# Norm sums in two fp32r passes, softmax's last product on GpSimd, and consecutive splits of queries and keys

## The reference

```python
def rmsnorm_2(x, g):
    xf = x.astype(jnp.float32)
    y = xf * lax.rsqrt(jnp.mean(xf * xf, axis=-1, keepdims=True) + EPS)
    return (y * g.astype(jnp.float32)).astype(x.dtype)
...
q_ca = rmsnorm_2(hs(q_ca, N_CA_HEADS), g_q[l])
k_ca = rmsnorm_2(hs(k_ca, N_CA_HEADS), g_k[l])
...
s = jnp.einsum('bnqhd,bnkhd->bnhqk', qc, k_band).astype(jnp.float32) * (d ** -0.5)
s = s + bias[None, None]
p = jax.nn.softmax(s, axis=-1)
out = jnp.einsum('bnhqk,bnkhd->bnqhd', p.astype(v.dtype), v_band)
```

## Time and profile before

| | |
|---|---|
| median of three runs | 955.28 us (955.16 to 955.39) |
| the profiled execution | 955.42 us |
| its span in the profile | 953.7 us |
| busy: TensorE, VectorE, ScalarE, GpSimd | 941.1, 691.2, 565.2, 103.8 us |
| granted TensorE clock | 1.0 throughout, the upper level of 2.4 GHz |
| steps 0 to 63 | about 393 to 453 us |

### The profile page before, as it was taken

One profiled execution on the slowest core, in us unless ns is written; L12 is line 12 of the kernel. 1 busy time (PEld: TensorE's weight loads), 2 busy tenths in 40 slices (PEclk: granted clock), 3 DMA queues, 4 the chain that ended last, 5 costly groups with the idle time before them and its releaser, 6 DMA issues.

```text
span 953.7 us, 13305 instructions
## 1 busy us (share of the span) xinstructions
PE 941.1 (99%) x4712; PEld 786.3 (82%) x4712; DVE 691.2 (72%) x1278; ACT 565.2 (59%) x1115; POOL 103.8 (11%) x215
## 2 busy tenths in 40 slices
PE   8999999999999999999999999999999999999998
PEld 7878998888888887877788877898888888888887
DVE  6487888878788766667768886856544853673988
ACT  6448787753223257479987664556745634644562
POOL 5001212211121103000000000110000000000110
PEclk9999999999999999999999999999999999999999
DMA  8233222149798743733442423365867567586773
GB/s 302 89 112 108 69 79 89 55 157 354 284 322 278 190 142 127 300 111 100 133 166 73 127 67 131 146 167 133 212 207 180 168 192 189 122 234 193 169 186 111
DMA packets 34963, 156.71 MB, mean 164 GB/s; under 512 B 5273, under 2 KB 5529, under 8 KB 22226
## 3 DMA queue, kind: packets, MB, share of 16 engines
q1 hardware_dynamic: 21106, 103.64, 31.6%
q0 software_dynamic: 11152, 49.29, 20.9%
q10 hardware_dynamic: 2640, 2.93, 0.9%
HBM read 144.61 MB, written 5.27 MB: 157 GB/s over the span
## 4 chain that ended last, share of the span: by engine, by line
PE 86%; DVE 9%; ACT 3%; issue 1%; DMA 1%; ACTq 0%; POOL 0%; DVEq 0%; POOLq 0%
PE psum L2276 26%; PE psum L2278 25%; PE psum L2277 25%; PE psum L2423 2%; PE psum L2450 2%; PE psum L2479 1%; PE psum L2474 1%; DVE wl L1318 1%; DVE p_sb L1518 1%; DMA raw<-in_wall 1%; DVE ptl L1537 1%; PE psum L2712 1%; DVE hl L1357 1%; DVE xt L1353 1%; DVE ah L1464 1%
## 5 line engine op out<-in xcount | busy, mean ns | idle before, releaser
L2276 PE MATMUL psum<-hh,wh 128*128 128x512 f32 (+2 forms) x736 | 277.7, 377 | 0.7 <-DVE hl L1357 0.6
L2278 PE MATMUL psum<-hh,wl 128*128 128x512 f32 (+2 forms) x736 | 270.2, 367 | 0.0
L2277 PE MATMUL psum<-hl,wh 128*128 128x512 f32 (+2 forms) x736 | 270.0, 367 | 0.0
L1318 DVE TENSOR_TENSOR wl<-raw,wh 128x512 fp32r<-128x512 f32 x336 | 218.7, 685 | 37.6 <-ACT wh L733 37.0
L733 ACT ACTIVATE wh<-raw 128x512 fp32r<-128x512 f32 x336 | 193.3, 621 | 68.3 <-PE psum L2278 65.2
L2276 PEld LDWEIGHTS psum<-hh,wh 128*128 128x128 f32 x736 | 138.5, 188 | 24.5 <-DVE hl L1357 1.8
L2278 PEld LDWEIGHTS psum<-hh,wl 128*128 128x128 f32 x736 | 138.4, 188 | 23.0
L2277 PEld LDWEIGHTS psum<-hl,wh 128*128 128x128 f32 x736 | 138.7, 188 | 20.5 <-issue 1.2
L2276 PE MATMUL psum<-wh,ah 128*128 128x512 f32 x192 | 76.1, 396 | 0.4 <-ACT p_sb L879 0.4
L2278 PE MATMUL psum<-wh,al 128*128 128x512 f32 x192 | 74.9, 390 | 0.0
L2277 PE MATMUL psum<-wl,ah 128*128 128x512 f32 x192 | 74.8, 389 | 0.0
(11 more groups left out here) (372 smaller groups left out, 1748.6 us busy)
## 6 DMA issues: line engine op xcount, KB each, us to landing
raw<-in_wall SPq DMA_DIRECT2D x79, 1024.0 KB, 5.4
raw<-in_wall POOLq DMA_DIRECT2D x20, 1024.0 KB, 8.1
wa<-in_wada POOLq DMA_DIRECT2D x24, 512.0 KB, 5.8
gt<-in_wada POOLq DMA_DIRECT2D x20, 512.0 KB, 6.9
xt<-in_xcols SPq DMA_DIRECT2D x8, 264.0 KB, 7.9
cb<-c_rows SPq DMA_DIRECT2D x8, 264.0 KB, 3.2
x<-in_x SPq DMA_DIRECT2D x4, 512.0 KB, 11.9
x_kept<-x SPq DMA_DIRECT2D x4, 512.0 KB, 2.6
```

What stands on the lines that cost most here:

```text
L1318: e.tensor_tensor(lower_, raw_of(w, c), upper_.bitcast(F32), ALU.subtract).then_inc(v["wl"], 1)
L2276: e.matmul(out_, lh, rh, start=start, stop=False, skip_group_check=True)
L2277: e.matmul(out_, lh, rl, start=False, stop=False, skip_group_check=True)
L2278: return e.matmul(out_, ll, rh, start=False, stop=stop, skip_group_check=True)
```

## The change

The sum of squares. `blk` becomes fp32r. After the square, ScalarE copies it to an fp32r tile `sq_hi`; two steps after the square (`LAG_LOW`) VectorE subtracts that from the square into `sq_lo`; and the sum is two fp32r matmuls, of the upper and of the lower part. `LAG_SUM`, `LAG_ROOT` and `LAG_NORM` go from 2, 3, 4 to 4, 5, 6 steps. Both new tiles exist once, so each waits for the sum before. They lie in memory that is free in this stage.

Softmax's last product goes from ScalarE to GpSimd for heads 8 to 15, five beats behind the scores and not six, and TensorE's transposes wait for GpSimd. GpSimd now walks the list of steps too, with its table masks, the row and the strip in between.

The splits of softmax heads' queries and keys stand in steps 6, 7, 8 and 9 on ScalarE (before 6, 8, 10 and 12) and in 7, 8, 9 and 10 on VectorE (before 7, 9, 11 and 13). Semaphores are renamed.

```diff
-        blk = sb("blk", [128, 128])
+        blk = sb("blk", [128, 128], F32R)
...
-        LAG_SUM, LAG_ROOT, LAG_NORM = 2, 3, 4
+        LAG_LOW, LAG_SUM, LAG_ROOT, LAG_NORM = 2, 4, 5, 6
...
-                if (x_ := at(AGE["norm"])) and x_[0] == "S" and x_[1] not in SB:
+                if (x_ := at(AGE["norm"])) and x_[0] == "S" and x_[1] in FG:
                     normalize(*x_[1:])
...
-                if 16 <= n < 80 and k in (6, 8, 10, 12):
-                    p, part = 3 + n // 16, (k // 2 - 3) % 2
-                    if k < 10:
+                if 16 <= n < 80 and k in (6, 7, 8, 9):
+                    p, part = 3 + n // 16, k % 2
+                    if k < 8:
...
                     e.activation(sq[:, sub, :], bank[sub], ACT.Square).then_inc(a["sq"], 1)
+                    e.wait_ge(a["sq"], 4 * p + 2 * sub + 1)
+                    if p or sub:
+                        e.wait_ge(t["ss"], 2 * p + sub)
+                    e.activation(sq_hi, sq[:, sub, :], ACT.Copy).then_inc(a["sq"], 1)
...
+                if n - LAG_LOW in SQUARES:
+                    p, sub = SQUARES[n - LAG_LOW]
+                    e.wait_ge(a["sq"], 4 * p + 2 * sub + 2)
+                    if p or sub:
+                        e.wait_ge(t["ss"], 2 * p + sub)
+                    e.tensor_tensor(sq_lo, sq[:, sub, :], sq_hi.bitcast(F32), ALU.subtract).then_inc(v["ss"], 1)
...
-                if 16 <= n < 80 and k in (7, 9, 11, 13):
-                    p, part = 3 + n // 16, (k // 2 - 3) % 2
-                    if k < 10:
+                if 16 <= n < 80 and k in (7, 8, 9, 10):
+                    p, part = 3 + n // 16, (k - 7) % 2
+                    if k < 9:
...
-            for h in CA:
+            def table_mask(h):
                 e.wait_ge(d[f"bt{h % 2}"], 16 * (h // 2 - 3))
                 e.memset(bt[h % 2][0:64, 448:512], NEG).then_inc(g["bt"], 1)
...
+            def normalize(h, i):
+                mx, su, nmx = small(h, i)
+                e.wait_ge(v["rcp"], n_score(h, i))
+                e.tensor_scalar(block_p(h, i), block_p(h, i), mx, None, ALU.mult).then_inc(g["norm"], 1)
+
+            table_mask(8)
+            table_mask(9)
+            for n in range(steps_s):
+                if n == 31:
+                    first_value_row()
+                if n == 72:
+                    whole_sticks()
+                if n > 16 and n % 16 == 1:
+                    for x_ in beats_s[first_s[n - 17]:first_s[n - 1]]:
+                        if x_ and x_[0] == "S" and x_[2] == 0 and x_[1] + 2 in CA:
+                            table_mask(x_[1] + 2)
+                for b_ in range(first_s[n], first_s[n + 1]):
+                    x_ = beats_s[b_ - 5] if b_ > 4 else None
+                    if x_ and x_[0] == "S" and x_[1] in CA:
+                        normalize(*x_[1:])
...
+                elif h in CA:
+                    e.wait_ge(g["norm"], 12 + n_score(h, i0) - 32)
                 else:
                     e.wait_ge(a["norm"], n_score(h, i0))
...
-                    e.wait_ge(a["sq"], 2 * p + sub + 1)
+                    e.wait_ge(v["ss"], 1 + 2 * p + sub + 1)
...
-                    e.matmul(bank[2], blk[:, :], sq[:, sub, :], start=True, stop=True).then_inc(t["ss"], 1)
+                    e.matmul(bank[2], blk[:, :], sq_hi, start=True, stop=False)
+                    e.matmul(bank[2], blk[:, :], sq_lo, start=False, stop=True).then_inc(t["ss"], 1)
```

More of the change, by code:

```diff
@@ L205, in program @@
         br.close()
+        bq = ExitStack()
+        sb("under_q", [128, 3072], where=bq)
+        parts_q = sb("sq_parts", [128, 2, SEQ], F32R, where=bq)
+        bq.close()
         gt = sb("gt", [128, 2, D])
@@ L278, in program @@
         sq = two
+        sq_hi, sq_lo = parts_q[:, 0, :], parts_q[:, 1, :]
         v_rows = (rows[:, 3072:3584], rows[:, 3840:4352], v_end[:, 0:512], rows[:, 1024:1536])
@@ L330, in program @@
                  "exp", "norm", "sig", "dv", "turn", "o", "oh", "mod")
-        v = sems("dve_", "wl", "acc", "ss0", "dg", "xn0", "hl0", "hn", "wfl", "v", "f", "scan", "crow", "cc", "za", "u", "y", "yz", "yl", "m",
+        v = sems("dve_", "wl", "acc", "ss", "dg", "xn0", "hl0", "hn", "wfl", "v", "f", "scan", "crow", "cc", "za", "u", "y", "yz", "yl", "m",
                  "ml", "tile", "mod", "ada", "x1", "yk", "xn1", "t1", "hl", "vca", "qn", "ql", "kl", "vsb", "x2", "xn2", "t2",
                  "s", "sl", "x3", "score", "max", "rcp", "scan_s", "dv", "turn", "o", "oz", "ol")
-        g = sems("pool_", "const", "meta", "rs0", "rs1", "rs3", "mask", "bt", "strip")
+        g = sems("pool_", "const", "meta", "rs0", "norm", "rs3", "mask", "bt", "strip")
         def home(w):
@@ L1034, in keep @@
             def keep(i):
-                e.wait_ge(g["rs1"], 3 * i + 3)
+                e.wait_ge(g["norm"], 3 * i + 3)
                 e.activation(x1[:, i, :], scaled[:, i % 2, :], ACT.Copy, scale=sm[:, 128 + 2 * i:129 + 2 * i]).then_inc(a["xk"], 1)
@@ L1394, in _ @@
             e.tensor_scalar(sm[0:META, 52:53], bank[4][0:META, 8:9], 1.0 / D, EPS, ALU.mult,
-                            ALU.add).then_inc(v["ss0"], 1)
+                            ALU.add).then_inc(v["ss"], 1)
             e.wait_ge(g["rs0"], 2)
@@ L2100, in _ @@
                             pattern=[[-1, 128]], channel_multiplier=1).then_inc(g["const"], 1)
-            e.memset(blk[:, :], 0.0).then_inc(g["const"], 1)
+            e.memset(blk[:, :].bitcast(F32), 0.0).then_inc(g["const"], 1)
             e.wait_ge(g["const"], 6)
-            e.memset(blk[0:64, 0:64], 1.0).then_inc(g["const"], 1)
-            e.memset(blk[64:128, 64:128], 1.0).then_inc(g["const"], 1)
+            e.memset(blk[0:64, 0:64].bitcast(F32), 1.0).then_inc(g["const"], 1)
+            e.memset(blk[64:128, 64:128].bitcast(F32), 1.0).then_inc(g["const"], 1)
             e.wait_ge(g["const"], 8)
@@ L2196, in _ @@
                 e.wait_ge(a["nsq"], 2 * i + 1)
-                e.tensor_scalar(r[:, 0:1], m1, EPS, None, ALU.add).then_inc(g["rs1"], 1)
+                e.tensor_scalar(r[:, 0:1], m1, EPS, None, ALU.add).then_inc(g["norm"], 1)
                 e.wait_ge(a["nsq"], 2 * i + 2)
[L2199 to L2202, removed]
+                e.wait_ge(g["norm"], 3 * i + 1)
+                e.tensor_scalar(r[:, 1:2], r[:, 0:1], EPS, m2, ALU.mult, ALU.add).then_inc(g["norm"], 1)
+                e.wait_ge(g["norm"], 3 * i + 2)
+                e.tensor_tensor(r, r, half[:, 0:2], ALU.pow).then_inc(g["norm"], 1)
             gate(0)
@@ L2206, in _ @@
             e.wait_ge(v["m"], 24)
-            for h in CA:
+            def table_mask(h):
                 e.wait_ge(d[f"bt{h % 2}"], 16 * (h // 2 - 3))
                 e.memset(bt[h % 2][0:64, 448:512], NEG).then_inc(g["bt"], 1)
[L2210 to L2222, removed]
+            def first_value_row():
+                for j in range(4):
+                    e.wait_ge(d[f"x{4 + j}"], 32)
+                e.wait_ge(v["tile"], 48)
+                e.memset(dv[0][0:1, :], 0.0).then_inc(g["strip"], 1)
@@ new lines, in whole_sticks @@
+            def whole_sticks():
+                e.wait_ge(v["qn"], 8)
+                e.wait_ge(v["tile"], 40)
+                e.memset(strip[:, 0:384], 0.0).then_inc(g["strip"], 1)
+                e.memset(strip[:, 384:512], 1.0).then_inc(g["strip"], 1)
+                e.wait_ge(g["strip"], 3)
+                e.affine_select(out=strip[:, 384:512], in_=strip[:, 384:512], compare_op=ALU.is_ge, fill=0.0, base=0,
+                                pattern=[[1, 128]], channel_multiplier=-1).then_inc(g["strip"], 1)
```

2 lines of the change are left out of this document (1 added, 1 removed).

## The result

The changed kernel takes 959.0 us (median of 9 runs, 957.05 to 960.59); the kernel before, on the same chip, 955.42 us (9 runs, 955.16 to 955.98). The ratio is 1.0034, with a 95% interval of 1.0025 to 1.0043: slower by a third of a per cent, where 1.65 us less was forecast. The nine runs stand in three groups by their mean granted clock: three at 1.000 (957.05 to 957.49 us), four at 0.998 (958.87 to 959.61 us), two at 0.996 (960.34 and 960.59 us). The profiled execution is one of the last: 960.34 us, a span of 958.6 us. The medians of the groups lie 1.95 and 1.45 us apart. So there are two losses to explain: 1.65 us (957.07 against 955.42) that every run has, and a clock loss that four runs have once and two, by their mean clock, twice.

A forecast was written before the change was run, and what follows sets the result against it. TensorE bounds the kernel, busy 941.1 of 953.7 us. Sums 2.8, first scores 0.8, early banks -0.2, transposes -0.3, step 68 -1.8, later wait +0.35 give 1.65 us: 955.42 - 1.65 = 953.8 us, range 951.5 to 956.7.

The forecast's parts named there:

- later wait: TensorE's 0.35 us wait before a matmul at 467.34 us goes as other engines catch up: 0.35 us won (0 to 0.5).
- step 68: Step of the hand-written order needing the bank the last norm frees; starts at 461.3, not 459.47 us: 1.8 us lost.
- The sums: Norm sums as two fp32r passes hold TensorE's line 0.46 us, not 0.86; seven of the eight win 2.8 us.
- the first scores: Before head 8's first scores, TensorE's 0.82 us wait for copies of split keys goes: 0.8 us won.
- Early banks: TensorE waits for banks that the later norms free: 0.2 us lost for all early banks (0 to 0.7).
- The transposes on GpSimd: TensorE's transposes wait for softmax's last product on GpSimd, taken as 0.85 us for 128x512: 0.3 us lost (0 to 2.5).
- the slower rival: "The chain does not fit its steps": squares queue on ScalarE, subtractions hold VectorE; 5.2 us lost at seven sums, 958.8 us; chance 0.15.
- What follows step 80 only shifts: After step 80 of the hand-written order, the work only moves in time; no term in the sum.

The follow-up runs named there:

- the version without the two waits: The changed kernel with the last sum one fp32 matmul at its old step and the last pair's splits every second step as before: 953.82 us, 0.9984.
- ten matmuls: The changed kernel plus ten 128x128 fp32 identity matmuls behind the last sum, result unread, so TensorE works while step 68 waits: 957.43 us, 1.0026.
- the kernel with one long wait (2.54 us): The changed kernel with only the last pair's splits put back to every second step: 956.8 us, 1.0012.

## Why the prediction was wrong, step by step

Two steps failed in their mechanism: "later wait", which the change lengthens where the prediction let it vanish, and step 68, whose price left out the clock that falls behind a wait. Ahead of them the right mechanisms were priced too low.

- **The sums** and **the first scores** were right: a pair holds the line 0.46 us, and the wait of the earlier trace rows is gone in the full change and in the splits alone.
- **Early banks:** 0.2 us forecast, 0.39 measured. Two matmuls that wait for a norm follow their predecessors late: that at 404.44 us by 0.34 instead of 0.23 us, that at 410.78 us by 0.51. The prediction had looked at the second place only.
- **The transposes on GpSimd** were the right mechanism with the wrong size: 0.3 us forecast, 0.94 measured (425.03 - 423.86 - 0.23). The term that failed is the product's duration, 0.85 us. GpSimd's eight products of 128x512 take 1.66 us in the mean:

```profile
L2244 POOL TENSOR_SCALAR p_sb<-p_sb,sm 128x512 f32<-128x512 f32 x8 | 13.3, 1664 | 49.7 <-DVE sm L1518 49.7
...
L2244 POOL TENSOR_SCALAR p_sb<-p_sb,sm 128x128 f32<-128x128 f32 x8 | 5.3, 665 | 2.4 <-DVE sm L1518 2.4
```

 A quarter of it, 128x128, takes 0.67 us, more than twice the mask of the earlier trace rows from which the estimate came. The mask was the wrong neighbour: it is another operation, and it reads no scalar from memory; which of the two makes the difference no run shows. The prediction's estimate by the Trainium skill (GPSIMD Engine Reference, section Engine selection), 1.38 us at the factor for two inputs, was nearer, and still too little.
- **Waits not in the sum:** 0.25 us before the seventh sum and 0.55 us at a copy of a transposed block (the matmul at 449.30 us follows one of 384 columns, 0.17 us, that starts at 448.58). The prediction named such queueing as the slower rival, at 0.75 us for each sum, and gave the forecast nothing of it. Of the 2.8 + 0.8 = 3.6 us won ahead of step 68 these terms and the two above take 2.1, where 0.5 was forecast; 1.5 us were left at 454 us.
- **Step 68** was right as to the wait: 1.8 us forecast with a wait of 2.5 to 3 us put down to the norm; 2.53 us measured, and 1.7 us in the balance. What the step did not price is what the stillness does to TensorE. The text of the step goes from the wait straight to "in that wait the other engines catch up". Behind it the granted clock fell to its half level, for a loss of 1.6 us in the profiled run; six of the nine runs had at least one such fall.
- **The later wait** failed in sign. It was to vanish (+0.35) because the others catch up. What the step missed stands in VectorE's rows: it looked at the wait of the earlier trace rows and not at what the change itself puts ahead of it: for the first pair the consecutive splits were followed through ScalarE and VectorE, for the last pair not at all. There they hold two weight parts back: 0.71 + 1.07 us where 0.35 had been, 1.4 us lost, and in part of the runs another fall of the clock. The splits alone and the run with the last pair spaced show it from both sides.
- **"What follows step 80 only shifts"** was right: from 474 us on all logits but one are 5.0 us late.

Together: forecast -1.65; 1.6 us less won ahead of step 68, 0.1 us less lost at it, 1.8 us more lost at the weight parts: +1.65, the 957.07 us of a run without a clock fall; with one, 959.0. The rival nearest in time, "the chain does not fit its steps", 958.8 us, comes nearer for the sums without the other two parts (957.45 us), where the longer chain does make TensorE wait, though at the first scores and at copies and not before the sums. It is not the cause here: the version without the two waits is 1.56 us faster than the kernel before. That this version's 953.82 us is the forecast's 953.8 is luck: it is another kernel, with other terms in its sum.

## What to carry to other kernels

When TensorE is 99% busy, price a new wait twice: its length, and the half clock that can follow it. When one pattern is applied to several groups, follow each group through its own queues: here three pairs of splits together gain 0.8 us and the fourth, whose splits hold back weight parts that TensorE waits for, loses 1.4 and brings falls of the clock. And a part that measures as nothing alone can be what makes another part pay.

## What the runs showed of the hardware

How often the clock fell, beside the waits of that part of the kernel (runs whose mean granted clock is 0.998 or less):

```
waits of TensorE, us                         runs with a fall
2.53 at step 68, then 0.71 and 1.07          6 of 9 (two of them at 0.996)
1.26, then 2.67 at step 68                   5 of 5 (one at 0.996)
2.54 at step 68                              6 of 11 (one at 0.996)
2.22 at step 68                              3 of 8
1.13 and 1.06, 2.0 us apart                  5 of 11
0.69 and 1.08, 2.0 us apart (ten matmuls)    3 of 9
0.68 and 1.07, 2.0 us apart                  2 of 11
all others, none over 1.70                   0 of 66 and, before, 0 of 88
```

The same program falls in one run and not in the next; why stays open, as does the run at 0.996 of the kernel with one long wait (2.54 us). Where the fall begins differs too. Behind step 68 of the changed kernel the step's own three matmuls, from 459.53 us, still run at full clock, those from 460.45 us on no longer; with the sums alone the first matmul behind that wait (463.38 us) already runs at half clock, the next one 0.59 us behind it, and so does the first behind the two waits near 470 us.

In the changed kernel GpSimd's products take from 0.60 us (128x128) to 1.95 us (128x512). Some of the longer ones fall beside a VectorE instruction with two inputs in SBUF: in the run with GpSimd alone a split that takes 0.69 us elsewhere took 1.07 at 433.64 us, and the product of 128x512 beside it 1.93. But not every such pair grows: the product of 128x512 at 446.00 us took 1.57, as short as any of that size, and the split beside it (446.73 us) its usual 0.69. What decides is open.
